# Alternating semaphore sets at phase borders, undivided row spreads, later ada chunks and an earlier second gated value in a two-block network kernel

## What is computed

```python
def _sublayer(x, fn, pre_g, post_g, shift, scale, gate, res_w):
    h = _rmsnorm(x, pre_g) * (1.0 + scale[:, None, :]) + shift[:, None, :]
    y = _rmsnorm(fn(h), post_g)
    return x + res_w * (1.0 + gate[:, None, :]) * y
```

## Time and profile before

| | us |
|---|---|
| median of 3 runs (3380.50 to 3382.39) | 3382.07 |
| the profiled execution | 3375.55 |
| its span on the core | 3373.7 |
| PE busy | 3100.2 (92%) |
| DVE busy | 1690.5 (50%) |
| POOL busy | 1346.1 (40%) |
| mean granted clock of PE, share of 2.4 GHz | 0.963 |

### The profile page before, as it was taken

How to read it: one execution, slowest core, us unless ns; L and a number is a source line. 1 busy time by engine, 2 the same in 40 slices (tenths; PEclk the granted TensorE clock), 3 DMA queues, 4 the chain that set the end, 5 groups by cost and what they waited for, 6 DMA issues and landing times. The chain is left out here.

```text
span 3373.7 us, 52883 instructions
## 1 busy us (share of the span) xinstructions
PE 3100.2 (92%) x20203; PEld 2492.3 (74%) x20203; DVE 1690.5 (50%) x3186; ACT 1160.0 (34%) x2080; POOL 1346.1 (40%) x885
## 2 busy tenths in 40 slices
PE   5999989899999999999999988996788899979997
PEld 4888865688887888877788867874566666758875
DVE  6444477655445672234771115426567755263343
ACT  3222235322223222244322223234444434243442
POOL 3444442334444444443434432224677740233332
PEclk8999999999999999999999999997899999979998
DMA  7655421265554553322453332222222243122221
GB/s 219 195 178 179 131 73 56 75 193 180 177 155 140 176 174 91 96 85 67 143 162 93 98 97 81 67 92 65 49 58 58 54 108 114 32 72 70 70 62 44
DMA packets 636806, 365.37 MB, mean 108 GB/s; under 512 B 107326, under 2 KB 629172, under 8 KB 636112
## 3 DMA queue, kind: packets, MB, share of 16 engines
q1 hardware_dynamic: 628816, 351.42, 35.7%
q10 hardware_dynamic: 6640, 10.49, 1.0%
q0 software_dynamic: 1168, 0.91, 0.1%
HBM read 333.67 MB, written 24.90 MB: 106 GB/s over the span
## 5 line engine op out<-in xcount | busy, mean ns | idle before, releaser
L262 POOL TENSOR_TENSOR w_lo<-w_raw,w_hi 128x1024 fp32r<-128x1024 f32 (+1 forms) x386 | 914.0, 2368 | 1681.6 <-ACT w_hi L254 1638.8
L254 ACT ACTIVATE w_hi<-w_raw 128x1024 fp32r<-128x1024 f32 (+1 forms) x386 | 401.6, 1041 | 951.1 <-PE acc L327 683.6
L327 PE MATMUL acc<-h,w_hi 128*128 128x512 f32 x2256 | 705.9, 394 | 8.1 <-DVE v_padded L1721 8.1
L327 PEld LDWEIGHTS acc<-h,w_hi 128*128 128x128 f32 x2256 | 418.2, 188 | 93.6 <-DVE v_padded L1721 8.5
L327 PE MATMUL acc<-h,w_lo 128*128 128x512 f32 x1128 | 440.9, 391 | 0.0
L327 PE MATMUL lat<-h,w_hi 128*128 128x512 f32 x912 | 332.9, 405 | 24.6 <-DVE h L498 18.3
L327 PE MATMUL acc<-hid,w_hi 128*128 128x512 f32 x1056 | 326.4, 390 | 0.0
L1048 DVE SCALAR_TENSOR_TENSOR ada_part<-ada_raw,c_act,ada_part 128x256 f32<-128x256 f32 x672 | 315.0, 489 | 18.6
L327 PEld LDWEIGHTS acc<-h,w_lo 128*128 128x128 f32 x1128 | 212.0, 188 | 45.8
L327 PEld LDWEIGHTS acc<-hid,w_hi 128*128 128x128 f32 x1056 | 197.3, 188 | 40.5
L327 PEld LDWEIGHTS lat<-h,w_hi 128*128 128x128 f32 x912 | 172.5, 192 | 71.4 <-DVE h L498 13.7
(11 more groups left out here) (620 smaller groups left out, 5665.9 us busy)
## 6 DMA issues: line engine op xcount, KB each, us to landing
w_raw<-in_ffn_w SPq DMA_DIRECT2D x240, 512.0 KB, 4.0
ada_raw<-in_ada_w SPq DMA_DIRECT2D x88, 1024.0 KB, 5.0
w_raw<-in_od_w_in SPq DMA_DIRECT2D x32, 512.0 KB, 4.1
w_raw<-in_ev_w_in SPq DMA_DIRECT2D x30, 512.0 KB, 3.9
w_raw<-in_ffn_w SPq DMA_DIRECT2D x32, 384.0 KB, 3.5
image<-inverse_wait SPq DMA_DIRECT2D x144, 64.0 KB, 2.2
first_ada<-in_ada_w SPq DMA_DIRECT2D x8, 1024.0 KB, 12.4
w_raw<-in_ab_w_in SPq DMA_DIRECT2D x16, 512.0 KB, 4.0
```

What stands on the lines that cost most here:

```text
L254: act.activation(K.w_hi[:, first % SPLIT, 0:tiles, :], K.raw[:, first % RAW, 0:tiles, :], ACT.Copy).then_inc(K.hi_ready, 1)
L262: pool.tensor_tensor(K.w_lo[:, first % SPLIT, 0:tiles, :], K.raw[:, first % RAW, 0:tiles, :], K.w_hi[:, first % SPLIT, 0:tiles, :].bitcast ...
L327: mm = pe.matmul(out, w[:, slot, k, :], moving(ap, k, tokens), start=first and k == 0 and p == 0, stop=last and k == tiles - 1 and p == le ...
```

## The change

Eight edits, in the order of the text below:

1. The end of a phase: POOL alone clears the semaphores of the phase, and the next phase uses a second set of 60.
2. The reciprocal is done in one piece of 128 columns, and PE spreads it with four matmuls of 128 columns in place of eight of 64 (in `start_phase`, in `quick_pre_pe` and in `border_pe`).
3. `run_on` of 4 behind the border's spread is gone, and `run_on` ahead of the next phase's spread is 6 calls in place of 5.
4. Ada chunks move one turn later in phases 0, 2 and 3, and two turns later in phase 5; phases 0 and 2 take one more with the down product.
5. `load_ahead` and `weights_sp` follow: four raw chunks may come from two segments.
6. `gated(1)` stands behind tap 9 of `conv_b(0)`.
7. In PE's 31 taps, `mean(2)` moves from behind tap index 1 to 11, `var(2)` from 8 to 17, `spread(0)` from 16 to 24, `spread(1)` from 20 to 30 and `spread(2)` from 26 to behind the last.
8. `lru_scale` follows from edit 4: its place is n = 7 in place of n = 6.

```diff
 def load_ahead(sp, K, phase):
-    seg = phase[0]
-    for i in range(RAW // seg.per):
-        load_turn(sp, K, seg, i, i)
-    if seg.ada:
-        load_ada(sp, K, seg, 0, 0)
+    left = RAW // phase[0].per
+    for seg in phase:
+        out = min(left, seg.n)
+        for i in range(out):
+            load_turn(sp, K, seg, i, i)
+        if out and seg.ada:
+            load_ada(sp, K, seg, 0, 0)
+        left -= out
 def weights_sp(sp, K, index, ahead=True):
-    for k, seg in enumerate(K.weights.phases[index]):
-        out = RAW // seg.per if k == 0 else 0
+    left = RAW // K.weights.phases[index][0].per
+    for seg in K.weights.phases[index]:
+        out = min(left, seg.n)
+        left -= out
...
-            loop(sp, out, seg.n, RAW // int(np.gcd(RAW, seg.per)), turn)
+            lead = ADA if seg.ada_base + out < FIRST_ADA + ADA and seg.ada_n else out
+            for i in range(out, lead):
+                turn(i, i)
+            loop(sp, lead, seg.n, RAW // int(np.gcd(RAW, seg.per)), turn)
-def spread_halves(pe, K, out, rows, ready):
-    for h in range(2):
-        pe.wait_ge(ready, h + 1)
-        for c in range(4):
-            mm = pe.matmul(out[:, c * P + 64 * h:c * P + 64 * h + 64], K.ident[:, 32 * c:32 * c + 1].broadcast_to([P, P]),
-                           rows[:, 64 * h:64 * h + 64], start=True, stop=True)
+def spread_rows(pe, K, out, rows, ready):
+    pe.wait_ge(ready, 1)
+    for c in range(4):
+        mm = pe.matmul(out[:, c * P:(c + 1) * P], K.ident[:, 32 * c:32 * c + 1].broadcast_to([P, P]), rows[:],
+                       start=True, stop=True)
     return mm
...
-    run_on(pe, K, spare, 5)
-    spread_halves(pe, K, K.spare, K.root_next, S.next_inv).then_inc(S.factors, 1)
+    run_on(pe, K, spare, 6)
+    spread_rows(pe, K, K.spare, K.root_next, S.next_inv).then_inc(S.factors, 1)
     run_on(pe, K, spare, 6)
...
-        halves_dve(dve, K.root_next, S.next_inv)
+        dve.reciprocal(K.root_next[:], K.root_next[:]).then_inc(S.next_inv, 1)
...
     run_on(pe, K, spare, 3)
-    spread_halves(pe, K, K.sums, K.root, S.post.rstd_ready)
-    run_on(pe, K, spare, 4)
+    spread_rows(pe, K, K.sums, K.root, S.post.rstd_ready)
...
-    nc.all_engine_barrier(sems_to_clear=range(K.local0, K.local0 + K.local_n))
+    nc.gpsimd.sem_clear(range(K.local0, K.local0 + K.local_n))
+    K.local0, K.other0 = K.other0, K.local0
...
-                    lead = 2 if done == 0 else 0
+                    lead = min(max(2 - done, 0), part.n)
...
-                    if k == 1:
+                    if k == 11:
                         mean(2)
-                    elif k == 8:
+                    elif k == 17:
                         var(2)
-                    elif k == 16:
+                    elif k == 24:
                         spread(0)
-                    elif k == 20:
+                    elif k == 30:
                         spread(1)
-                    elif k == 26:
-                        spread(2)
                 mm.then_inc(S.conv_ps, 1)
+                spread(2)
                 mean(HB - 1)
...
                 gated(0)
-                done = conv_b(0, done)
-                gated(1)
+                done = conv_b(0, done, {8: lambda: gated(1)})
                 done = conv_b(1, done)
...
-        W.add(*ffn_weights(0, 0, [(22, ada1(0, 8))], ada1(0, 30), 6))
+        W.add(*ffn_weights(0, 0, [(1, None), (21, ada1(0, 8))], ada1(0, 29), 7))
...
-        W.add(*ffn_weights(0, 1, [(22, ada1(1, 0))], ada1(1, 22), 7))
-        W.add(*ffn_weights(1, 0, [(7, ada1(1, 29)), (12, ada2(0, 0)), (3, None)]))
+        W.add(*ffn_weights(0, 1, [(1, None), (21, ada1(1, 0))], ada1(1, 21), 8))
+        W.add(*ffn_weights(1, 0, [(1, None), (7, ada1(1, 29)), (12, ada2(0, 0)), (2, None)]))
...
-        W.add(*ffn_weights(1, 1, [(12, ada2(1, 0)), (10, None)]))
+        W.add(*ffn_weights(1, 1, [(2, None), (12, ada2(1, 0)), (8, None)]))
```

More of the change, by code:

```diff
@@ L627, in spread_pe @@
     return mm
-def spread_halves(pe, K, out, rows, ready):
-    for h in range(2):
-        pe.wait_ge(ready, h + 1)
-        for c in range(4):
-            mm = pe.matmul(out[:, c * P + 64 * h:c * P + 64 * h + 64], K.ident[:, 32 * c:32 * c + 1].broadcast_to([P, P]),
-                           rows[:, 64 * h:64 * h + 64], start=True, stop=True)
-    return mm
-def halves_dve(dve, rows, ready):
-    for h in range(2):
-        dve.reciprocal(rows[:, 64 * h:64 * h + 64], rows[:, 64 * h:64 * h + 64]).then_inc(ready, 1)
+def spread_rows(pe, K, out, rows, ready):
[3 more added lines that the diff above has]
+                       start=True, stop=True)
+    return mm
 BORDER_SEMS = ("p_ready", "x_ready", "next_root", "next_inv", "factors", "x_own", "z_added", "crossed", "cross_added",
@@ L812, in border_dve @@
     dve.wait_ge(S.post.std_ready, 1)
-    halves_dve(dve, K.root, S.post.rstd_ready)
+    dve.reciprocal(K.root[:], K.root[:]).then_inc(S.post.rstd_ready, 1)
     step = K.root_next[:]
@@ L816, in border_dve @@
     dve.wait_ge(S.cross_done, 1)
-    dve.wait_ge(S.post.rstd_ready, 2)
+    dve.wait_ge(S.post.rstd_ready, 1)
     math(dve.tensor_tensor(step, bank[:, 0:P], K.root[:], ALU.mult))
@@ L1179, in _ @@
                 mm.then_inc(S.x_summed, 1)
-                spread_halves(pe, K, K.spare, K.root_next, S.root_inv)
+                spread_rows(pe, K, K.spare, K.root_next, S.root_inv)
                 for m in range(FIRST_ADA):
@@ L1203, in _ @@
                         dve.wait_ge(S.root_ready, 1)
-                        halves_dve(dve, K.root_next, S.root_inv)
+                        dve.reciprocal(K.root_next[:], K.root_next[:]).then_inc(S.root_inv, 1)
                     if m >= 2:
@@ L1722, in gated, with conv_b @@
                                       ALU.mult).then_inc(S.v_ready, 1)
-                def conv_b(b, done):
+                def conv_b(b, done, beside={}):
                     dve.wait_ge(S.v_ready, v_order.index(b) + 1)
@@ L1740, in conv_b @@
                         done += 1
+                        if k in beside:
+                            beside[k]()
                     dve.wait_ge(S.conv_b, done)
@@ L3967, in build @@
         K.local_n = 60
-        local = [nc.alloc_semaphore(name=f"local{i}") for i in range(K.local_n)]
-        K.local0 = local[0].num
-        assert [h.num for h in local] == list(range(K.local0, K.local0 + K.local_n))
+        local = [nc.alloc_semaphore(name=f"local{i}") for i in range(2 * K.local_n)]
+        K.local0, K.other0 = local[0].num, local[K.local_n].num
+        assert [h.num for h in local] == list(range(K.local0, K.local0 + 2 * K.local_n))
         for h in local:
```

## The result

| | before | after |
|---|---|---|
| median, us | 3382.23 (3380.50 to 3383.22) | 3351.69 (3348.43 to 3353.48) |
| ratio, 95% interval | | 0.9913 (0.9901 to 0.9925) |
| profiled execution / span | 3375.55 / 3373.7 | 3350.3 / 3348.5 |
| mean granted clock | 0.963 | 0.964 |

The change takes 0.87% (30.5 us) off. The forecast of 3350.7 lies 1 us from the median, but the sum behind it was made against the profiled execution, and there the difference is 25.2 us where the sum said 31.4. The rest is that the profiled execution of before lay 6.7 us under its median and that of after 1.4 us under its own. So the sum was 6.2 us too good, and the table shows where. That the median still came within 1 us of the forecast is luck: most of this error was made up by where the two profiled executions happened to lie.

The account below looks back on a forecast made before the run. PE's matmuls bound feed-forward phases, an ACT, DVE and PE chain the borders, DVE and ACT the layer-0 mixer's last third. Gains of 35.05 less 0.85, 0.6 and 2.2 gave 31.4 us off the median: 3350.7, range 3339 to 3363.

Parts of the forecast that it names:

- Second meeting gone: Phase ends: engines other than POOL start at the Block's release, 8.3 us won; 0.85 lost again in phase 4.
- The border: Five phase borders: one-piece reciprocal and spread end the Block earlier, 5.8 us, and start DVE earlier after it, 2.5 us.
- The rival of the low clock at the borders: Without `run_on` of 4, each border costs 16 us more through 1.2 GHz matmuls, 3431 us in all; chance 0.03.
- Start phase: Start phase: shorter spread at the 1.2 GHz level, less a later start, wins 1.45 us.
- Ada chunks: Phases 2, 3 and 5: PE's stalls and low clock in early turns go, 14.4 us; phase 2's border loses 0.6.
- the rival that the stall moves: Ada stall only moves to turn 1; some 2.4 of 14.4 us remain, 3362.7 us; chance 0.10.
- `lru_scale` (minus 2.2): End of phase 0: the later start and one step held by POOL cost 2.2 us, bounds 0 and 2.6.
- The mixer: Layer-0 mixer: PE gains 10 us, but late `mean(2)` leaves only 2.6 us at the end, bounds 0.5 and 10.
- The rival that the whole gain arrives: Layer-0 mixer: PE's position sets the end, so 10 us stand in place of 2.6, 3343.3 us; chance 0.15.
- Its own signs: Trace marks expected after the change, among them mixer 3 to 6 us shorter and borders some 2.4 us shorter each.

Follow-up runs that it names:

- e4: Kernel before with only the phase-end edit (POOL alone clears, two semaphore sets in turns): 3370.17 us, ratio 0.9977.
- e7: Kernel before with only reciprocal and spread in one piece and no `run_on` of 4 behind the border's spread: 3369.46 us, ratio 0.9971.
- e6: Kernel before with only the later ada chunks, their loads and `lru_scale` at n = 7: 3373.91 us, ratio 0.9992.
- e9: Kernel before with only the later ada chunks and their loads, `lru_scale` staying at n = 6: 3369.22 us, ratio 0.9971.
- e2_lru_6: Changed kernel with `lru_scale` at n = 6 instead of n = 7: 3350.67 us, ratio 0.9916.
- e5_mean_alone: Changed kernel with only `mean(2)` back behind tap index 1, the other four places staying late: 3345.2 us, ratio 0.9912.
- e3: Kernel before with only `gated(1)` behind tap 9 and the five new places between PE's taps: 3379.26 us, ratio 1.0000.
- e8: Changed kernel with the five old places, `lru_scale` at n = 6, and POOL's phase 4 loads behind its first differences and sums: 3340.29 us, ratio 0.9893.
- e11: Changed kernel with unread matmuls (`run_on` of 12, 13 and 4) in PE's three pauses ahead of phase 1's output product: 3348.83 us, ratio 0.9910.
- e1: Changed kernel with the five old places of the group sums between PE's 31 taps: 3344.57 us, ratio 0.9905.
- e12: Kernel before with only `gated(1)` moved behind tap 9, the five tap places left: 3369.05 us, ratio 0.9965.
- e10: Changed kernel with the five old places and `lru_scale` at n = 6, POOL's phase 4 loads left in place: 3341.14 us, ratio 0.9888.

## Why the prediction was right, and where its sum was off

**Second meeting gone (8.3, less 0.85): right.** 0.70 us a phase in e4 against 0.74, and 7.8 us by its ratio. In phase 4 PE waits 0.9 us for POOL's `m`, which takes back 0.8 of what DVE won; POOL being late showed in the chunk's low part and not in `x`, where the earlier trace rows had pointed.

**The border (5.8 and 2.5): right.** In the changed kernel the last product to the Block's end went from 6.11 to 4.91 us in phase 3 (1.16 predicted, though its own two ends, 438.44 and 439.63, make 1.19), by 0.90 in phases 1, 2 and 4 (in phase 2 with a chunk's matmuls added). In e7 the five borders together gave 5.4 of the 5.8. The Block's end to the first product went from 6.38 to 5.23, so 1.15 against 1.24 for meeting and border together. By its ratio e7 gave 9.8 us, where 5.8, 2.5 and 1.45 made 9.75. The rival of the low clock at the borders had its best case in e7 and did not come.

**Start phase (1.45): right,** 1.31.

**Ada chunks (14.4, less 0.6): right.** The waits in turn 0 are gone, turn 1 has one of 0.18 us (0.44 predicted) at granted clock 1.00, and the rival that the stall moves fell. Alone, phases 2, 3 and 5 gave 3.6 to 3.7, 2.1 and 7.0 to 8.0 us (e6 and e9), 12.8 to 13.7 in all; the terms made 2.4, 3.0 and 8.4, 13.8 in all: too small by 1.2 in phase 2, too large in the others. In phase 5 the waits for later chunks came to 3.1 us in the changed kernel and 2.0 in e2_lru_6, with the same code there: such waits vary by a microsecond between executions.

**`lru_scale` (minus 2.2): its time was right, its follow-up was missed.** Nine steps, one hold of 2.30, the end at 436.38: 2.27 us late, as worked out. What no term had was PE at the lower level behind the wait of 2.41, which made the spread 1.91 us long and the end of the Block wait for PE: from the last product to the end 3.1 us more than with n = 6 (e2), 2.27 of it the late step and 0.8 the clock. In e5_mean_alone, with the same code here and the same wait of 2.41 us, no low clock followed; the spread took 1.06 us and the way to the Block's end was 2.4 us longer than with n = 6, which is the late step without the clock.

```profile
435.30 0.43 PE L618 MATMUL scaled<-sq,const 128*32 128x128 f32 x8 [2.41 <-DVE sq L793]
436.43 1.06 PE L642 MATMUL sums<-norm_roots,const 128*128 128x128 f32 x8
```

Beside the other border, in e6, the same lateness cost three times as much. This term should have had a range open to the side of loss: PE idle for 2.4 us ahead of a chain that PE is part of.

The step held here is a TENSOR_SCALAR, as in the earlier trace rows. In e2_lru_6 the first held step was a TENSOR_TENSOR with two inputs, so both forms are held. The two engines there:

```profile
417.84 2.40 POOL L270 TENSOR_TENSOR w_lo<-w_raw,w_hi 128x1024 fp32r<-128x1024 f32 x1 [1.67 <-ACT w_hi L262]
417.93 2.33 DVE L1229 TENSOR_TENSOR lam<-lam 128x4 f32<-128x4 f32 x1
```

The Trainium skill, "GPSIMD Engine Reference", section Specifications, states that GpSimd contends with VectorE's instructions that have two SBUF inputs; the row of this TENSOR_TENSOR agrees. The prediction had 2.4 by that page and 2.2 by its rows, and 2.27 was measured.

**The mixer (2.6): right in kind, the term with the largest error in size.** The prediction had the mechanism: the 10 us arrive on PE, `mean(2)` stands 8.8 us later, and DVE's wait grows. Measured 0.5 (e3 0.55). Of the 3.1 that the prediction let through, `mean(2)` was to bring 1.2; it brought 0.13. PE's convolution began 1.3 us later than calculated (by 108.25 and 1.15 for the border against 108.1), because the gate matmuls ran at the lower level; in e8, where they don't, it begins at 107.04, which with the 1.15 is 108.2. The other 1.0 us was lost between `mean(2)` and the last `normal`. There the clock ahead of the output product had 0.5 in the term. e11 measured 3.1 for the whole stretch; but the kernel before has 3.4 us at the lower level there as well (its stretch 594.60 to 598.10 below), and one of that length cost 1.5 in e1, so the change added some 1.6, an estimate from these two.

```profile
594.60:598.10 3.50, 3.50 (x13) 2.72 (x10) 0.95 (x1) 2.51 (x3) 0.00 (x0) 0.52 0.00 0
```

The rival that the whole gain arrives was wrong for this change, but it is what edit 6 does alone: 8.5 in e12.

The prediction also took the five places for one delay at `mean(2)`. They are several in a row: with `mean(2)` back alone, DVE comes to stand at `spread(0)` (e5).

**Phase 0's front:** the first product came 0.73 us earlier and turn 0 had no chunk any more, but `multiply_fourth` ended only 0.19 us earlier in the phase, since the clock rose at 62.3 us as before; from there to the last product it took 351.9 us in place of 351.1, with the chunk that was put with the down product. The prediction had counted the 0.74 as won and the chunk at nothing: 1.3 us. The first half of this varies from one execution to the next: with the same code `multiply_fourth` ended at 27.60 us in the changed kernel and at 26.07 in e5, where the clock rose earlier; the 351.9 us are the same within 0.1 in all runs with the moved chunks. **Phase 4:** 3.4 us at the lower level at 1550 us, absent in e2 (172.75) and in the kernel before (173.97), took some 1.6 more; without it 1.2 us are won, where 1.55 were predicted. **The second block** shortened by 6.4 us against 3.9, but in the changed kernels of the experiments phases 6 to 9, with the same code in each, took between 1341 and 1354 us together, so 2.5 us there are no finding.

**Its own signs.** No drain, no wait in turn 0, none for L1721 and over 10 us for `mean(2)` came as listed. Two did not: the mixer was to get 3 to 6 us shorter and got 2.55, and the borders, from the last product to the first of the next phase, were to get 2.4 us shorter each and got 2.05 to 2.35; at phase 0, where the list has 0.9 (its terms, 2.4 less 2.2, make 0.2), the border got 0.75 us longer.

## What to carry to other kernels

When an operation that another engine waits for is shifted within a stream, list every wait of that other engine behind it, and read for each whether it has slack: moving `gated(1)` ahead was worth 8.5 us, and moving five small PE operations to later places behind it lost 8.0 of them. Where an edit makes PE stand for 2 us or more ahead of dense work or of a chain it is part of, price the lower clock as a term of its own with a wide upper end. Judge parts of some microseconds by the length of their own phase, since the median of the whole moves by as much through phases that nobody touched.

## What the runs showed of the hardware

The same wait of PE (2.4 us, at the same place of the program) was followed by none at the lower level in e5_mean_alone, by 3.4 us in the changed kernel and by 17 us in e6_ada_turns. The same code of phase 1 ran with 6.8 us at the lower level in e10 and with none in e8. So the clock behind a pause can't be read off the pause alone. Matmuls that nobody reads, 29 calls that take 7.2 us in all, put into 9.8 us of pauses, delayed nothing that can be seen and won 3.1 us; why one pause is followed by a long stretch and another by a short one was not settled.
